# The first loads of a transformer layer cut into pieces in order of use, and its gate columns multiplied as a 32-column stationary side

## The reference

```python
def reference(x, mem, w_in, ...):
    h = hybrid_mixer(x, w_in[l], ...)           # proj = x @ w_in, 3592 columns, split into
                                                # gq gk gv gz | gb ga (4 + 4 gate columns) | dq dk dv
    x = layer_norm(DEEPNORM_ALPHA * x + h, ...)
    h = mem_cross_attention(x, mem, ...)
    x = layer_norm(DEEPNORM_ALPHA * x + h, ...)
    h = moe_ffn(x, ...)                         # top 4 of 32 experts, 3 matrices 1024x1024 each
    x = layer_norm(DEEPNORM_ALPHA * x + h, ...)

# in hybrid_mixer
beta = jax.nn.sigmoid(gb.astype(f32))
g = -jnp.exp(a_log.astype(f32)) * jax.nn.softplus(ga.astype(f32) + dt_bias.astype(f32))
```

## Time and profile before

| | us |
|---|---|
| median of 3 runs | 1304.68 (1303.6 to 1306.26) |
| the profiled execution's own time | 1308.02 |
| span of the profiled execution, first to last instruction | 1306.3 |
| PE busy | 1256.5 (96%) |
| weight loads busy | 589.3 (45%) |
| VectorE busy | 331.2 (25%) |
| ScalarE busy | 282.8 (22%) |
| DMA, mean rate over the span | 342 GB/s |

### The profile page before, as it was taken

The page is one execution under the profiler, slowest core; times in us unless marked ns, Lnnn a source line. Parts: engine busy times, 40 slices in busy tenths (PEclk is TensorE's granted clock), DMA queues, the critical chain, the costliest instruction groups (busy, mean ns, idle before and its releaser), DMA issues.

```text
span 1306.3 us, 15882 instructions
## 1 busy us (share of the span) xinstructions
PE 1256.5 (96%) x5875; PEld 589.3 (45%) x5876; DVE 331.2 (25%) x935; ACT 282.8 (22%) x501; POOL 46.6 (4%) x39
## 2 busy tenths in 40 slices
PE   7999999999989999999999999999999999998994
PEld 6878796685533333333333333333333333333331
DVE  1652252320421122211222112221112212111115
ACT  0231233111112122121221212212122211221121
POOL 0103101000100000000000000000000000000001
PEclk9999999999889999999999999999999999999998
DMA  8650404058769994999999999999999999999992
GB/s 312 229 208 7 189 1 169 35 227 335 303 264 426 430 427 180 429 427 430 427 430 428 427 429 428 428 429 427 429 428 428 429 428 429 428 428 429 428 429 85
DMA packets 42903, 446.83 MB, mean 342 GB/s; under 512 B 6768, under 2 KB 7104, under 8 KB 18304
## 3 DMA queue, kind: packets, MB, share of 16 engines
q1 hardware_dynamic: 39312, 441.50, 80.5%
q10 hardware_dynamic: 3568, 5.01, 1.2%
HBM read 445.44 MB, written 1.05 MB: 342 GB/s over the span
## 4 chain that ended last, share of the span: by engine, by line
PE 77%; DMA 19%; issue 2%; DVE 1%; POOL 0%; another core or an unknown queue 0%; SPq 0%; POOLq 0%; ACT 0%; DVEq 0%; ACTq 0%
PE bank L1240 28%; DMA main<-in_exp_w_up_dram 19%; PE bank L1283 13%; PE bank L828 8%; PE bank L818 5%; PE bank L1213 3%; PE bank L1181 3%; PE bank L1255 3%; PE bank L1047 2%; PE bank L1187 1%; PE bank L869 1%; PE bank L959 1%; PE bank L966 1%; PE bank L859 1%; PE bank L964 1%
## 5 line engine op out<-in xcount | busy, mean ns | idle before, releaser
L1240 PE MATMUL bank<-main 128*64 128x512 f32 x2112 | 478.4, 604 | 20.9 <-DMA main<-in_exp_w_up_dram 16.3
L1240 PEld LDWEIGHTS bank<-main 128*64 128x64 f32 x2112 | 154.5, 139 | 313.7 <-issue 309.7
L1283 PE MATMUL bank<-main,kst 128*64 128x512 f32 x1056 | 241.1, 598 | 0.0
L1691 DVE TENSOR_TENSOR main<-bank,main 128x256 f32<-128x256 f32 x66 | 28.1, 425 | 588.2 <-PE bank L1255 588.2
L772 ACT ACTIVATE main<-bank 128x512 f32<-128x512 f32 x66 | 39.4, 597 | 430.5 <-PE bank L1240 430.5
L1283 PEld LDWEIGHTS bank<-main,kst 128*64 128x64 f32 x1056 | 69.9, 136 | 122.9 <-issue 118.6
L828 PE MATMUL bank<-main 128*128 128x512 f32 x256 | 111.9, 592 | 0.3 <-ACT main L648 0.3
L818 PE MATMUL bank<-main 128*128 128x256 f32 x352 | 77.9, 380 | 0.0
L828 PEld LDWEIGHTS bank<-main 128*128 128x128 f32 x256 | 47.9, 190 | 56.1 <-issue 55.9
L818 PEld LDWEIGHTS bank<-main 128*128 128x128 f32 x352 | 66.3, 190 | 10.2 <-issue 1.5
L1213 PE MATMUL bank<-main 64*128 64x512 f32 x272 | 67.6, 615 | 0.7 <-ACT main L781 0.7
(11 more groups left out here) (247 smaller groups left out, 855.1 us busy)
## 6 DMA issues: line engine op xcount, KB each, us to landing
main<-in_exp_w_gate_dram SPq DMA_DIRECT2D x64, 2048.0 KB, 30.1
main<-in_exp_w_up_dram SPq DMA_DIRECT2D x64, 2048.0 KB, 34.5
main<-in_exp_w_down_dram SPq DMA_DIRECT2D x64, 2048.0 KB, 32.9
main<-in_w_in_dram SPq DMA_DIRECT2D x7, 2048.0 KB, 27.8
main<-in_xa_wk_dram SPq DMA_DIRECT2D x2, 2048.0 KB, 10.9
main<-in_w_out_dram SPq DMA_DIRECT2D x2, 2048.0 KB, 11.3
main<-in_xa_wv_dram SPq DMA_DIRECT2D x2, 2048.0 KB, 10.7
main<-in_xa_wq_dram SPq DMA_DIRECT2D x2, 2048.0 KB, 13.2
```

The source lines that it names most:

```text
L1240: last = pe.matmul(gu_bank[f][64 * side:64 * side + 64, :], xg_chunk(k), weights(role, k, f), start=(k == 0), stop=(k == KC - 1))
L1283: last = pe.matmul(y_bank[64 * h:64 * h + 64, :], hT[:, k, :], weights(role, k, h), start=(k == 0), stop=(k == KC - 1))
L1691: tt(mg[:, f, :, :], gT[:, :, 0, :], bias(0), ALU.add)
```

## The change

The first loads are issued in smaller pieces and in another order, and PE takes the work in the order in which the pieces come.

- x is loaded in four pieces of 256 KB, the two of the first 128 tokens by SP and the two of the last 128 by ACT. ACT loads the identity ahead of them, apart from the other constants. PE transposes in the order xT0, xT2, xT1, xT3 (xT0 and xT2 hold the first four contraction blocks of all tokens), each behind its own piece.
- w0 comes in four loads of 512 KB, one for each contraction block, right behind x. The loop of its products has the contraction block outside and the unit inside.
- The load of the gate columns and of the two gate parameters stands behind w0 on SP's queue, and PE's products of them stand behind the products of w0.
- The gate columns are padded with zeros to 32 (GpSimd clears the place first), and are the stationary side, with the 256 tokens moving. The eight contraction blocks go to four column tiles of the array, two to each, so that PSUM holds four partial sums on 128 partitions. VectorE copies them to SBUF, and two more products with a 128 x 8 matrix of ones and zeros (ba_pick, from a sum over the identity) add them and turn them back to tokens on partitions. These stand behind the first four products of w1.

```diff
@@ unit_table @@
-    u = [(f"xT{i}", "D") for i in range(4)] + [("ba", "D"), ("columns", "D")]
+    u = [(f"xT{i}", "D") for i in (0, 2, 1, 3)] + [("ba", "D"), ("columns", "D")]
@@ trunk_kernel @@
+        w_ba = dqk[:, 0:256].rearrange("p (k n) -> p k n", k=KC)
+        ba_parts = dqk[:, 256:512]
+        ba_pick = dqk[:, 512:520]
@@ sync @@
-            sp.dma_start(x3, d["x"][0].rearrange("(b p) n -> p b n", p=P)).then_inc(ld_x, 16)
-            ba_dst = dnw_keep[:, 0:64].rearrange("p (k n) -> p k n", k=KC)
-            sp.dma_start(ba_dst, d["w_in"][0, :, C_BA:C_BA + 8].rearrange("(k p) n -> p k n", p=P)).then_inc(ld_ba, 16)
+            for h in range(2):
+                sp.dma_start(x3[:, 0, h * HALF:(h + 1) * HALF], d["x"][0, 0:P, h * HALF:(h + 1) * HALF]).then_inc(ld_x[h], 16)
+            for k in range(4):
+                sp.dma_start(slots[0][:, k, :], d["w_in"][0, k * P:(k + 1) * P, C_QK:C_QK + 1024])\
+                    .then_inc(ring_full[0] if k == 3 else ld_first[k], 16)
+            sp.wait_ge(ba_zero, 1)
+            sp.dma_start(w_ba[:, :, 0:8], d["w_in"][0, :, C_BA:C_BA + 8].rearrange("(k p) n -> p k n", p=P)).then_inc(ld_ba, 16)
             sp.dma_start(a_log, d["gdn_a_log"][0:1, :].partition_broadcast(P)).then_inc(ld_ba, 16)
             sp.dma_start(dt_b, d["gdn_dt_bias"][0:1, :].partition_broadcast(P)).then_inc(ld_ba, 16)
             for i, (name, col, cols, half) in enumerate(ATTENTION_LOADS):
+                if i == 0:
+                    continue
@@ gpsimd @@
+            pool.memset(dqk[:, 0:256], 0.0).then_inc(ba_zero, 1)
             pool.memset(cin[:, :, 0:PAD], 0.0).then_inc(pad_zero, 1)
@@ scalar @@
-            act.dma_start(kst[:, :], d["consts"][:, 0:N_CONST]).then_inc(ld_const, 16)
+            act.dma_start(ident, d["consts"][:, K_ID:K_ID + P]).then_inc(ld_ident, 16)
+            for h in range(2):
+                act.dma_start(x3[:, 1, h * HALF:(h + 1) * HALF], d["x"][0, P:SEQ, h * HALF:(h + 1) * HALF]).then_inc(ld_x[2 + h], 16)
+            act.dma_start(kst[:, K_ID + P:N_CONST], d["consts"][:, K_ID + P:N_CONST]).then_inc(ld_const, 16)
@@ tensor @@
-            pe.wait_ge(ld_const, 16)
-            pe.wait_ge(ld_x, 16)
-            for i in range(4):
+            pe.wait_ge(ld_ident, 16)
+            for i in (0, 2, 1, 3):
+                pe.wait_ge(ld_x[i], 16)
                 transpose_block(f"xT{i}", x3[:, i // 2, :], range(4 * (i % 2), 4 * (i % 2) + 4))
-            need("xT2", "xT3")
+
+            w = through(0, 1)
+            need("xT2")
+            for k in range(KC // 2):
+                if k < 3:
+                    pe.wait_ge(ld_first[k], 16)
+                else:
+                    arrived(0)
+                for i in range(4):
+                    ps = begin(f"qk{i}") if k == 0 else bank(f"qk{i}")
+                    pe.matmul(ps[:, 0:SEQ], w(k)[:, 2 * i * P:(2 * i + 1) * P], xT[:, k, :], start=(k == 0), stop=False)
+
+            need("xT3")
             pe.wait_ge(ld_ba, 48)
             ps = begin("ba")
-            for b in range(TB):
-                for k in range(KC):
-                    last = pe.matmul(ps[:, 8 * b:8 * b + 8], xT[:, k, b * P:(b + 1) * P], dnw_keep[:, 8 * k:8 * k + 8],
-                                     start=(k == 0), stop=(k == KC - 1))
-            last.then_inc(unit_filled, 1)
-
-            w = through(0, 1)
-            arrived(0)
-            for i in range(4):
-                ps = begin(f"qk{i}")
-                for k in range(KC // 2):
-                    pe.matmul(ps[:, 0:SEQ], w(k)[:, 2 * i * P:(2 * i + 1) * P], xT[:, k, :], start=(k == 0), stop=False)
+            for k in range(KC):
+                c = k % 4
+                last = pe.matmul(ps[32 * c:32 * c + 32, 0:SEQ], w_ba[:, k, :], xT[:, k, :], start=(k < 4), stop=(k >= 4))
+            last.then_inc(ba_parted, 1)
             pe.wait_ge(ld_cols, 80)
-            ps = begin("columns")
-            pe.transpose(ps[:, 0:80], columns_raw, ident[0:80, 0:80]).then_inc(unit_filled, 1)
+            columns_ps = begin("columns")
+            pe.transpose(columns_ps[:, 0:80], columns_raw, ident[0:80, 0:80])
             arrived(1)
             for i in range(4):
                 ps = bank(f"qk{i}")
                 for k in range(KC // 2, KC):
                     pe.matmul(ps[:, 0:SEQ], w(k)[:, 2 * i * P:(2 * i + 1) * P], xT[:, k, :], start=False, stop=(k == KC - 1))
+                if i == 0:
+                    pe.wait_ge(ba_copied, 1)
+                    pe.wait_ge(ba_picked, 1)
+                    for b in range(TB):
+                        last = pe.matmul(bank("ba")[:, SEQ + 8 * b:SEQ + 8 * b + 8], ba_parts[:, b * P:(b + 1) * P], ba_pick,
+                                         start=True, stop=True)
+                    last.then_inc(unit_filled, 2)
@@ vector @@
-            for i in range(4):
+            dve.wait_ge(ld_ident, 16)
+            dve.reduce_sum(ba_pick, ident.rearrange("p (c n) -> p n c", c=4)[:, 0:8, :], AX_X).then_inc(ba_picked, 1)
+            for i in (0, 2, 1, 3):
                 dve.tensor_copy(xT[:, 4 * (i % 2):4 * (i % 2) + 4, (i // 2) * P:(i // 2 + 1) * P], as3(filled(f"xT{i}"), 4)).then_inc(dve_emptied, 1)
 
+            dve.wait_ge(ba_parted, 1)
+            dve.tensor_copy(ba_parts, bank("ba")[:, 0:SEQ]).then_inc(ba_copied, 1)
             ps = filled("ba")
-            dve.tensor_copy(ba, ps[:, 0:16]).then_inc(dve_emptied, 1)
+            dve.tensor_copy(ba, ps[:, SEQ:SEQ + 16]).then_inc(dve_emptied, 1)
             dve.tensor_copy(columns, filled("columns")[:, 0:80]).then_inc(dve_emptied, 1)
```

More of the change, by code:

```diff
@@ L353, in trunk_kernel @@
         ring_used = sem("ring_used")
-        ld_x, ld_const, ld_lev, ld_mem, ld_vec, ld_ba = (sem(n) for n in ("ld_x", "ld_const", "ld_lev", "ld_mem", "ld_vec", "ld_ba"))
+        ld_x = [sem(f"ld_x{i}") for i in range(4)]
+        ld_first = [sem(f"ld_first{k}") for k in range(3)]
+        ld_ident = sem("ld_ident")
+        ld_const, ld_lev, ld_mem, ld_vec, ld_ba = (sem(n) for n in ("ld_const", "ld_lev", "ld_mem", "ld_vec", "ld_ba"))
+        ba_zero, ba_picked = sem("ba_zero"), sem("ba_picked")
+        ba_parted, ba_copied = sem("ba_parted"), sem("ba_copied")
         ld_ln = sem("ld_ln")
```

## The result

The kernel after takes 1315.23 us (median of 20 runs) against 1304.66 for the kernel before on the same chip (20 runs, 1302.42 to 1309.41). Three of the 20 runs of after (1636, 4232 and 4514 us) were disturbed and are left out of the ratio, which is 1.0061, with a 95% interval of 1.0042 to 1.008; the median of the other 17 is 1312.71 us. I had forecast 1304.4, with 1307.6 as the upper end and "slower" at 0.17. The 17 fall into two groups, 8 at 1307.86 to 1309.67 and 9 at 1312.71 to 1320.86; both lie above the range. The profiled execution belongs to the second, with an own time of 1317.27 us.

What follows compares the result with a forecast made beforehand. The prediction took PE's opening chain and w1's landing as the bound, the landing being decisive. Its sum, - 3.4 (w1 earlier) + 2.2 (clock) + 0.9 (summing product) = -0.3 us, gave 1304.4 us, range 1301.0 to 1307.6.

Steps and rivals of the forecast that it cites:

- T: Moment PE starts the products of w1, 28.69 us before; forecast 25.3, 3.4 us won, any shift reaching the kernel's end.
- PE's chain and the loads met at the same moment: In the opening, PE's work and w1's landing at 28.2 us coincide; shortening one alone gives 0.5 us.
- PE's own chain: PE's opening work without load waits: start about 5.5, w0 products to 18.4, at w1's wait by 20.6, 8 us earlier.
- The step that failed first: Small gate loads, moved behind w0 on SP's queue, end 2.2 us after it, at 16.7 us, in time for PE.
- So w1 lands at 25.2: Landing of w1's weights in the opening, 28.2 us before, was forecast at 25.2 (bounds 23.4 and 28.5).
- The 1.7 us that I had counted as won from the slow stretch: DMA stretch from 7.2 to 9.0 us at 17 GB/s lacks 0.71 MB; winning it back brings w1 1.7 us earlier.
- Slower: w1 lands no earlier: Small loads' slow stretch now straight ahead of w1: 2.7 to 3.5 us slower, 1307.8; chance 0.14.
- The rival of dear pieces: Gaps of 1.3 us between small load pieces delay w1 by 5 us: 4.7 us slower, 1309.4; chance 0.03.
- The third wait: Sign of a slower kernel: PE waits for gate loads or a late w0 piece, pushing it past w1's landing.
- What the wait costs: PE idle 4.7 us ahead of w1 lowers its clock; w1's first products run at half rate, losing 2.2 us.
- The gates: Gates start 2.5 to 3.5 us later in the opening; two units of convolution absorb the delay, costing nothing.
- From there on both kernels have the same work in the same order, but for four small instructions: After w1's products start, the work is unchanged but for four small instructions, so a shift there reaches the end.

Runs made afterwards that it cites:

- held_padded: The changed kernel with ACT's vectors, mem and masks held until the gate loads landed, plus six unused small PE products (24 instructions): 1297.23 us, ratio 0.9932.
- tiles_padded: The kernel before with only the gate product on four column tiles and its summing product, plus six unused small PE products: 1304.68 us, ratio 1.0005.
- act_held: The changed kernel with ACT issuing its other vectors, mem and masks only once the three gate loads are in: 1304.64 us, ratio 0.9989.
- after_padded: The changed kernel plus six unused small PE products, bringing PE's program back to its old length: 1308.59 us, ratio 1.0023.
- before_fewer: The kernel before with six filler products late in the attention part left out, 24 PE instructions fewer, opening untouched: 1310.92 us, ratio 1.0049.
- loads_only: The changed kernel with the old gate product (16 products of 8 columns) at the new place, PE's old number of instructions: 1312.02 us, ratio 1.0062.
- after_again: The changed kernel measured again without any edit: 1312.32 us, ratio 1.0061.
- held_gates_early: The changed kernel with ACT's later loads held, six unused PE products added, and the gate loads ahead of w0's pieces: 1302.88 us, ratio 0.9982.
- before_short: The kernel before with gate sums over 5 of 8 contraction blocks, 24 PE instructions fewer in the opening, changing the gates: 1336.17 us, ratio 1.0222.
- gates_early: The changed kernel with the three gate loads put back behind x and ahead of w0's four pieces: 1308.61 us, ratio 1.0023.
- tiles_only: The kernel before with only the gate product on four column tiles, its copy and summing product, all loads as before: 1313.62 us, ratio 1.0064.

## Why the prediction was wrong

**What bounds the kernel.** That T goes through to the end is right: held_padded wins 7.4 us at T and 7.5 in the span. That PE's chain and the loads met at the same moment is right too: tiles_padded, with the faster gate product, has T earlier by the 0.5 us that I had named for shortening one alone, and gains nothing in the end.

**PE's own chain.** Right. Start at 4.5 (predicted 5.5, bounds 4 and 7.9), w0's products ended at 18.6 (18.4), with one wait of 1.84 us for the fourth piece of x that I hadn't counted. The gate product takes 1.94 us at the lower clock (2.0 taken) and 1.07 at the full one; the summing product 0.51 (0.9 taken).

**The step that failed first** reads: "The small loads now come behind it and end 2.2 us later (10.0 against 7.8 above), at 16.7, also in time." They ended at 25.1. I moved three loads in time and kept their duration, but that duration belonged to an emptier neighbourhood: from 7.2 to 9.0 us of the kernel before, ACT's queue moved 92 packets and SP's 298, and where the change puts the loads they take turns with ACT's packets, 716 against 711 in six microseconds. act_held shows it. With it fell "So w1 lands at 25.2 (bounds 23.4 ... and 28.5)": it landed at 30.2. The 1.7 us that I had counted as won from the slow stretch became a slow stretch of six microseconds at 65 GB/s. My rival "Slower: w1 lands no earlier" had the right mechanism, the small loads' slow stretch straight ahead of w1, and too small a price: it put T near 28.3, and T was 30.2 and 31.4 in the two profiles. The rival of dear pieces had nearly the right T, 30.3, for the wrong reason: x's and w0's pieces went at 377 GB/s. The third wait that I named as a sign ("for the gate loads ... that pushed PE past w1's landing") did come, but w1 was later still.

**What the wait costs.** Right in kind, smaller than I had said: the low stretch lasted to 33.1, and w1's first 8 instructions took 3.40 us instead of 1.93, 1.5 us against the 2.2 in my sum. With the summing product's half microsecond that turns 1.5 us at T into 3.4 at v0. The clock and the summing product together cost 1.9 us where I had 3.1; the error of the sum lies in T, forecast as 25.3 and measured as 30.2.

**How far the first step goes.** It is enough by itself to leave the range: the shorter group of the runs of after, and after_padded with 1308.59, lie above 1307.6.

**The gates.** Right that they cost nothing: VectorE has them at 39.79 (39.10 + 0.69) instead of 34.6, which is 5.2 us later and not 3, yet the second convolution starts at 39.99 against 39.92, and its wait of 1.55 us has shrunk to 0.20.

**The term that was missing.** "From there on both kernels have the same work in the same order, but for four small instructions" took it for granted that the same work takes the same time. The change makes PE's program 24 instructions shorter, and with that the code for the second half of the expert loop is more often asked for too late. Taking 24 instructions out elsewhere (before_fewer) and putting them back (held_padded) show the effect of the length; loads_only shows that it is not the only condition. The late fetch costs 6 us or more in the executions it hits (before_fewer), more than the opening's 4 to 5. No part of the sum could have held it: the rows of before showed no long stall there.

**What stays open.** Why the request comes early in one execution and late in the next, with the same code (after_again against after), why held_gates_early is mostly long although it is padded, why loads_only is in half of its runs, and why before_short has the short stall in its profile. gates_early, with 2.46 us, lies between the two cases. tiles_only's profile has the short stall and is its fastest but one run, so its median of 1313.6 is laid to the long stall only because padding took 9 us off, 1.7 of them in the opening. No profile shows the long stall in that kernel.

## What to carry to other kernels

Loads of hundreds of tiny pieces have no duration of their own: before moving one, look at what the other queues have under way where it will stand, and place it where they are idle, or hold them back. Shortening a long unrolled program with loops can move the fetch of a later block of code, as it seems to have done here; where the time changes far from the edit, compare the "issue" waits of both profiles, and run a version padded to the old length. A saving in a part should be tested with that padding, or it can be taken for a loss (tiles_only, 1.0064, against tiles_padded, 1.0005).

## What the hardware showed that I had not expected

- 1024 pieces of 32 bytes beside another queue's small packets: dt_bias, which is queued behind them, took 15.5 us, and 5.0 with that queue held back.
- The issue of a 2 KB load (a_log) behind many pieces held SP for 5.14 and 5.54 us, with every later load behind it.
- Products of 32 weight columns and 256 moving columns on four column tiles are 0.067 us apart at the full clock (1.07 / 16) and 0.12 at the lower one (1.94 / 16). All sixteen come close to the 0.9 us that was my lower bound.
- PE goes on some 4.5 us after the packet with its 16 KB of code starts, and 24 instructions more or fewer ahead of the loop, in the opening or late in the attention part, moved the median by 4 to 9 us with everything else nearly as it was.
